# A two-block transformer kernel: the feed-forward stages multiply the un-normalised residual, the root scales the products, and the final norm is fused with the norm after it

## The reference

```python
def rmsnorm(x, g):                       # over the 1024 channels of a token
    return x * rsqrt(mean(x * x) + 1e-6) * g

# first block, two layers, 528 tokens
for l in range(2):
    h = h + hybrid_mixer(rmsnorm(h, norm_mix_g[l]), ...)
    u = causal_dwconv(rmsnorm(h, norm_ffn_g[l]) @ w_up, conv_w, conv_b)   # 3 taps, 2 * 2816 columns
    gate, val = split(u)
    h = h + (silu(gate) * val) @ w_down
x = rmsnorm(h, final_norm_g)[:, 16:]     # 512 tokens from here on

# second block, two layers
for i in range(2):
    x = x + 0.5 * swiglu(rmsnorm(x, ffn1_norm[i]))      # silu(x @ gate) * (x @ up) @ down
    x = x + (attention if i == 0 else gmlp)(rmsnorm(x, mix_norm[i]))
    x = x + 0.5 * swiglu(rmsnorm(x, ffn2_norm[i]))
```

## Time and profile before

| | |
|---|---|
| median of three runs | 3935.97 us (3935.6 to 3939.99) |
| the profiled execution, first to last instruction (span) | 3934.8 us |
| TensorE matmul busy | 3699.1 us, 94% |
| VectorE busy | 1606.4 us, 41% |
| ScalarE busy | 1146.4 us, 29% |
| GpSimd busy | 1323.0 us, 34% |
| HBM read | 291.00 MB, 74 GB/s over the span |

### The profile page before, as it was taken

How to read it: one execution, slowest core, us unless ns; L and a number is a source line. 1 busy time by engine, 2 the same in 40 slices (tenths; PEclk the granted TensorE clock), 3 DMA queues, 4 the chain that set the end, 5 groups by cost and what they waited for, 6 DMA issues and landing times.

```text
span 3934.8 us, 55367 instructions
## 1 busy us (share of the span) xinstructions
PE 3699.1 (94%) x20874; PEld 3152.2 (80%) x20874; DVE 1606.4 (41%) x2221; ACT 1146.4 (29%) x1622; POOL 1323.0 (34%) x530
## 2 busy tenths in 40 slices
PE   7999899999998999899998878999999989899999
PEld 7994899989948999878876656788788868777887
DVE  4343542442535424541348765313431353634131
ACT  4332332323323323222222242222221222522222
POOL 3210344433202444334433201444344434333443
PEclk9996999999968999899999978999999999999999
DMA  3210232322101233223332201233233323222333
GB/s 109 59 44 1 70 99 83 93 71 72 43 7 54 86 91 93 73 75 96 95 87 59 69 1 43 85 96 92 79 96 92 99 82 91 74 76 79 96 94 93
DMA packets 570031, 294.79 MB, mean 75 GB/s; under 512 B 10663, under 2 KB 568230, under 8 KB 569782
## 3 DMA queue, kind: packets, MB, share of 16 engines
q1 hardware_dynamic: 568724, 291.39, 25.5%
q0 software_dynamic: 768, 1.11, 0.1%
q10 hardware_dynamic: 418, 0.62, 0.1%
HBM read 291.00 MB, written 2.10 MB: 74 GB/s over the span
## 4 chain that ended last, share of the span: by engine, by line
issue 46%; PE 42%; POOL 9%; DVE 1%; ACT 1%; POOLq 0%; DMA 0%; SPq 0%; ACTq 0%; DVEq 0%
PE big L1638 35%; POOL wlow L613 9%; PE misc L1809 1%; PE big L1674 1%; PE misc L1792 1%; PE big L1912 1%; PE misc L1897 1%; PE misc L1687 0%; PE misc L1698 0%; POOLq L175 0%; PE misc L1802 0%; DVE fresh L1167 0%; DVE acc L1114 0%; DVE xlow L1151 0%; PE misc L1806 0%
## 5 line engine op out<-in xcount | busy, mean ns | idle before, releaser
L613 POOL TENSOR_TENSOR wlow<-raw,whigh 128x1024 fp32r<-128x1024 f32 (+1 forms) x508 | 1312.8, 2585 | 2580.0 <-ACT whigh L627 2579.9
L1638 PE MATMUL big<-xhigh,whigh 128*128 128x264 f32 (+1 forms) x4176 | 1218.9, 337 | 1.9 <-POOL wlow L613 1.3
L1638 PE MATMUL big<-xlow,whigh 128*128 128x264 f32 (+1 forms) x4176 | 1214.1, 336 | 0.0
L1638 PE MATMUL big<-xhigh,wlow 128*128 128x264 f32 (+1 forms) x4176 | 1209.5, 335 | 0.0
L627 ACT CAST whigh<-raw 128x1024 fp32r<-128x1024 f32 (+1 forms) x508 | 563.6, 1110 | 2145.8 <-PE big L1638 2087.2
L1638 PEld LDWEIGHTS big<-xhigh,whigh 128*128 128x128 f32 x4176 | 713.7, 189 | 94.8 <-issue 7.7
L1638 PEld LDWEIGHTS big<-xlow,whigh 128*128 128x128 f32 x4176 | 711.7, 189 | 86.7 <-issue 5.6
L1638 PEld LDWEIGHTS big<-xhigh,wlow 128*128 128x128 f32 x4176 | 712.3, 189 | 80.7
L1638 PE MATMUL big<-ffn_hidl,whigh 128*128 128x264 f32 (+1 forms) x1408 | 421.4, 340 | 0.0
L1638 PE MATMUL big<-ffn_hidh,wlow 128*128 128x264 f32 (+1 forms) x1408 | 420.9, 339 | 0.0
L1638 PE MATMUL big<-ffn_hidh,whigh 128*128 128x264 f32 (+1 forms) x1408 | 419.0, 338 | 0.0
(11 more groups left out here) (301 smaller groups left out, 3100.2 us busy)
## 6 DMA issues: line engine op xcount, KB each, us to landing
raw<-in_ffn_w_gate_up SPq DMA_DIRECT2D x176, 512.0 KB, 3.8
raw<-in_ffn_w_down SPq DMA_DIRECT2D x96, 704.0 KB, 4.6
raw<-in_ffn_w_up SPq DMA_DIRECT2D x88, 512.0 KB, 3.8
raw<-in_w_in SPq DMA_DIRECT2D x52, 512.0 KB, 3.9
raw<-in_gmlp_w_in SPq DMA_DIRECT2D x32, 512.0 KB, 4.0
raw<-in_attn_w_in SPq DMA_DIRECT2D x24, 512.0 KB, 3.7
raw<-in_w_out SPq DMA_DIRECT2D x16, 512.0 KB, 3.9
raw<-in_gmlp_w_out SPq DMA_DIRECT2D x16, 512.0 KB, 3.9
```

The lines of the kernel that those rows point to most:

```text
L613: eng.tensor_tensor(wlow[:, at0:at0 + n], raw[:, at0:at0 + n], whigh[:, at0:at0 + n].bitcast(F32), ALU.subtract).then_inc(slab_split, 1)
L1638: mm = eng.matmul(wide(big, slot, T)[:, c:c + n], w[:, (s * KC + k) * P:(s * KC + k + 1) * P], x[:, (x0 + k) * width + c:(x0 + k) * width ...
```

## The change

- Which x a stage multiplies. In the six feed-forward stages the operand is h times the gain of the norm, without the root. ScalarE makes its rounded part with the gain as scale, VectorE the rest, for each tile as soon as `residual` has written it (`after_residual`, `low_of`). Since the stage before may still read `xhigh`, stages behind mix, attn or gmlp use new buffers `x2h`, `x2l`; the others use `xhigh`, `xlow`.
- Where the root comes in. `first_pair` now holds the means (ahead of step 6) and the spread (ahead of step 8), and VectorE runs root and copy without the eight rounds. In cffn each product is scaled in PSUM before the convolution starts (`u_scaled`); ScalarE waits for that. In ffn VectorE scales gate and other half into `sg` and `pr`; ScalarE applies silu in place; the product has both inputs in SBUF.
- The final norm. While the last cffn adds to h, two sums of squares are formed: of h, and of h times the final gain (`acc2`). `final_root` gets both roots from them, one after the other, and spreads two rows: the first block's root, and the product of both roots. The operand of the next ffn is h times the product of both gains (`S_FG`, made once at the start). h itself is scaled after the first loop body of that ffn (eight operations), before its second.
- mix, attn and gmlp keep their norms as they were; only counts of `fresh_ready` are shifted.

Core of the diff:

```diff
+MEANS_AT, SPREAD_AT = 6, 8
...
+        x2h = rg.sb("x2h", KD * T1, F32R)
+        x2l = rg.sb("x2l", KD * T1, F32R)
...
+            def after_residual(n, k, s, tiles_done):
+                m = next_of(n)
+                if m is None:
+                    return
+                T = norm_T[norm_of[m]]
+                final = plan[m - 1][0] == "final"
+                eng.wait_ge(tile_out[s], tiles_done)
+                squares_free(norm_of[m], k)
+                if final and (not isinstance(k, int) or k >= 2):
+                    eng.wait_ge(summed2, k)
+                if m in x_of:
+                    eng.activation(c1(x_of[m][0], k, T), hc(k, T), ACT.Identity, scale=gain(m, k)
+                                   ).then_inc(xhigh_ready, 1)
+                squares_of(norm_of[m], k, s, T)
+                if final:
+                    eng.activation(c1(fresh, s, T), hc(k, T), ACT.Square, scale=pdyn("final_norm_g", None, k)
+                                   ).then_inc(squared2, 1)
...
-                        eng.wait_ge(slab_done, up.base + 2 * i + 1)
...
+                            eng.wait_ge(u_scaled, 2 * (first + i) + 1)
...
-                            eng.wait_ge(tile_out[1], tile0 // 2 + i)
-                            eng.activation(sg[:, 0:T], wide(big, 0, T), ACT.Silu).then_inc(tile_out[0], 1)
+                            eng.wait_ge(tile_out[0], tile0 // 2 + i + 1)
+                            eng.activation(sg[:, 0:T], sg[:, 0:T], ACT.Silu).then_inc(silu_ready, 1)
...
+            def low_of(n, k, T):
+                xh, xl = x_of[n]
+                eng.wait_ge(xhigh_ready, fill_of[n] + k + 1)
+                eng.scalar_tensor_tensor(out=c1(xl, k, T), in0=hc(k, T), scalar=gain(n, k),
+                                         in1=c1(xh, k, T).bitcast(F32), op0=ALU.mult, op1=ALU.subtract
+                                         ).then_inc(x_ready, 1)
+            def final_root(j):
...
+                root(rcol[:, 0:4], misc[:, 0:4], EPS, final_r, rcol2)
+                eng.wait_ge(final_r, 1)
+                chain(eng.tensor_tensor(rcol2[:, 8:12], rcol[:, 0:4], rcol[:, 0:4], ALU.mult))
+                chain(eng.tensor_tensor(rcol2[:, 12:16], rcol2[:, 8:12], misc[:, 4:8], ALU.mult))
+                root(rcol[:, 4:8], rcol2[:, 12:16], EPS, final_r, rcol2)
+                eng.wait_ge(final_r, 2)
+                eng.tensor_tensor(rcol[:, 8:12], rcol[:, 0:4], rcol[:, 4:8], ALU.mult).then_inc(rstd_ready, 1)
...
+                        if more and m in x_of:
+                            eng.wait_ge(tile_out[s], tile0 // 2 + i + 1)
+                            low_of(m, k, Tn)
...
+                        if final:
+                            eng.wait_ge(squared2, k + 1)
+                            eng.wait_ge(summed2, k + 1)
+                            eng.tensor_tensor(acc2[:, :], acc2[:, :], c1(fresh, s, T2), ALU.add).then_inc(summed2, 1)
...
+                                eng.wait_ge(slab_done, up.base + 2 * i + s + 1)
+                                eng.tensor_tensor(y, y, rstd[:, 0:T], ALU.mult).then_inc(u_scaled, 1)
...
-                            eng.wait_ge(tile_out[0], tile0 // 2 + i + 1)
+                            eng.wait_ge(slab_done, up.base + 2 * i + 1)
+                            eng.tensor_tensor(sg[:, 0:T], wide(big, 0, T), rstd[:, 0:T], ALU.mult).then_inc(tile_out[0], 1)
                             eng.wait_ge(slab_done, up.base + 2 * i + 2)
-                            val = wide(big, 1, T)
+                            eng.wait_ge(hid_ready, first + i)
+                            eng.tensor_tensor(pr[:, 0:T], wide(big, 1, T), rstd[:, 0:T], ALU.mult).then_inc(tile_out[1], 1)
+                            eng.wait_ge(tile_out[1], tile0 // 2 + i + 1)
+                            val = pr[:, 0:T]
+                        eng.wait_ge(silu_ready, first + i + 1)
...
                     body(0)
+                    if half == 0 and plan[n - 1][0] == "final":
+                        for k in range(KD):
+                            eng.scalar_tensor_tensor(out=hc(k, T2), in0=hc(k, T2), scalar=pcol("final_norm_g", None, k),
+                                                     in1=by_block(misc, 0, T2), op0=ALU.mult, op1=ALU.mult
+                                                     ).then_inc(final_done, 1)
+                        eng.wait_ge(final_done, KD)
                     repeat(eng, 1, HF, body)
...
                 for step in range(KD + LAG):
+                    if n is not None and step == MEANS_AT:
+                        norm_means(n)
+                    if n is not None and step == SPREAD_AT:
+                        norm_spread(n)
                     if step < KD:
                         eng.wait_ge(x_ready, q0 + step + 1)
...
             for n, ph in enumerate(plan):
-                norm_sum(norm_of[n])
                 if ph[0] != "final":
+                    if n not in x_of:
+                        norm_means(n)
+                        norm_spread(n)
```

More of the change, by code:

```diff
@@ L390, in build @@
                 continue
+            norms += 1
+            norm_T.append(T)
             fills += KD
+            unfresh[n] = KD * sum(p[0] in ("cffn", "ffn") for p in plan[:n])
+            if ph[0] in ("cffn", "ffn"):
+                gain_of[n] = ("norm_ffn_g", ph[1]) if ph[0] == "cffn" else (f"ffn{ph[1] % 2 + 1}_norm_2", ph[1] // 2)
+                x_of[n] = (x2h, x2l) if plan[n - 1][0] in ("mix", "attn", "gmlp") else (xhigh, xlow)
             if ph[0] == "mix":
@@ L425, in build @@
         final_done = sem("final_done")
-        z_ready = sem("z_ready")
+        z_ready, u_scaled = sem("z_ready"), sem("u_scaled")
+        squared2, summed2, final_step, final_r = [sem(x) for x in ("squared2", "summed2", "final_step", "final_r")]
         conv_step, silu_ready = sem("conv_step"), sem("silu_ready")
@@ L518, in parts, with gain, next_of @@
             return [(0, T // 2), (T // 2, T // 2)] if T == T1 else [(0, T)]
-        S_LB, S_OML, S_OMLS, S_SP, S_NSP, S_GQ, S_SUB, S_NLAM, S_TMP = 0, 8, 16, 24, 28, 32, 33, 34, 36
+        S_LB, S_OML, S_OMLS, S_SP, S_NSP, S_GQ, S_SUB, S_NLAM, S_TMP, S_FG = 0, 8, 16, 24, 28, 32, 33, 34, 36, 56
         def sm(c, n=1):
             return small[:, c:c + n]
+        def gain(n, k):
+            if plan[n - 1][0] == "final":
+                return small[:, ds(S_FG + k, 1)]
+            return pdyn(*gain_of[n], k)
+        def next_of(n):
+            m = n + 1
+            if m < len(plan) and plan[m][0] == "final":
+                m += 1
+            return m if m < len(plan) else None
         def load_slab(eng, st, s, i, n):
@@ L678, in one @@
                         ahead(x)
[L679 to L681 removed]
+                    after_residual(n, 2 * i + s, s, tile0 // 2 + i + 1)
                 def two(i):
@@ L712, in body @@
                             ahead(1)
-                            eng.wait_ge(slab_done, up.base + 2 * i + 2)
+                            eng.wait_ge(u_scaled, 2 * (first + i) + 2)
                             if done:
@@ L1018, in _ @@
                 if ph[0] == "final":
[L1020 to L1022 removed]
                     continue
                 T = norm_T[norm_of[n]]
[L1025 to L1026 removed]
+                for k in range(KD if n not in x_of else 0):
+                    split_fresh(n, fill_of[n] + k, c1(xhigh, k, T))
                 {"cffn": ffn, "ffn": ffn, "attn": attn, "gmlp": gmlp}[ph[0]](n, ph)
@@ L1185, in residual @@
             def residual(st, n, tile0, T, scale=None, bias=None, per_tile=1, last=True):
-                more = last and norm_of[n] + 1 < norms
+                m = next_of(n) if last else None
+                more = m is not None
+                final = more and plan[m - 1][0] == "final"
+                Tn = norm_T[norm_of[m]] if more else T
                 if more:
-                    clear_sum(norm_of[n] + 1, T)
+                    clear_sum(norm_of[m], Tn)
+                if final:
+                    eng.memset(acc2[:, :], 0.0).then_inc(summed2, 1)
                 def body(i):
@@ L1602, in _ @@
                 if ph[0] == "final":
-                    norm_root(norm_of[n], T1)
-                    more = norm_of[n] + 1 < norms
-                    if more:
-                        clear_sum(norm_of[n] + 1, T2)
-                    for k in range(KD):
-                        eng.scalar_tensor_tensor(out=hc(k, T2), in0=hc(k, T2), scalar=pcol("final_norm_g", None, k),
-                                                 in1=rstd[:, META:T1], op0=ALU.mult, op1=ALU.mult).then_inc(final_done, 1)
-                        if k and more:
-                            add_squares(norm_of[n] + 1, k - 1, (k - 1) % 2, T2)
-                    if more:
-                        add_squares(norm_of[n] + 1, KD - 1, 1, T2)
+                    final_root(norm_of[n])
                     continue
-                if ph[0] == "ffn":
```

(23 more changed lines are left out.)

96 lines of the change are left out of this document (55 added, 41 removed).

## The result

The changed kernel takes 3872.74 us (median of 4 runs, 3868.42 to 3874.97), the one before 3935.78 on the same chip: a ratio of 0.9838 [0.9825, 0.9852], 63.0 us less. The forecast was 3870.2, 65.8 less, with a range of 3856 to 3893.

What follows compares the result with a forecast made beforehand. The norm's chain ahead of the first matmul was taken to bound the six feed-forward entries. Savings of 16.2 us (two at 528 columns), 26.4 (three at 512) and 23.2 (final norm), together 65.8, gave 3870.2 us; range 3856 to 3893.

## What to carry to other kernels

A scale that is the same for a whole column of a product can be applied after it, and the reduction behind the scale then runs beside the matmuls; what that brings is the stretch in which TensorE stood still, and it holds only if the work added where each product is read out fits beside the matmuls, which doubling that work tests in one run. Once the chain is gone, look at what TensorE waits for next: here a wait for both weight slabs where only one was needed cost 3.76 us of idle time and 1.5 to 2.8 of low clock in each entry, nearly half as much again as the change brought. A chain of small operations on VectorE should be placed against GpSimd's long ones by time, not only by its own length.

## What the runs showed of the hardware

- An operation of VectorE on four columns, 0.16 us by itself, took 2.19 us when it started 0.17 us into GpSimd's 2.35 us `wlow`. The others of the same chain took 0.16 or 0.17. It ended with that `wlow`, within 0.01 us; so what it lost here was the rest of the other's instruction.
- A cast of 128x512 took 0.43 us alone and 2.49 us on average of 80 behind a `wlow`.
- After the same idle 3.76 us the clock was at 0.50 for 3 us in one execution and for over 5 in another, and the loss 1.36 or 2.76 us, with the same instructions. Fourteen unused products in the stall kept it at 1.00 there and made the entries 1.3 to 2.7 us shorter.
- One stretch of unchanged work took 115.71 us in one kernel and 118.48 in another, at granted clocks of 0.70 and 0.67.
